# Stream 0's output projection between stream 1's head groups, in the PSUM banks of its own transposes, and stream 1's norms of A further forward

## What is computed

```python
mod = (silu(cvec) @ ada_w[l] + ada_b[l])          # six parts: sh1, sc1, g1, sh2, sc2, g2
xn = rms_norm(x, norm1_g[l]) * (1 + sc1) + sh1
aq, ak, av, bq, ..., cq, ckv, ckr = split(xn @ w_in)
qa, ka = rms_norm(aq), rms_norm(ak)               # "norms of A"; rotary in stream 1
oa = attention(qa, ka, va, sink)                  # A: 6 heads of 64; stream 1 sees 128 cached tokens too
ob = mlstm_mixer(bq, bk, bv, bo, bg, ...)         # B: 4 heads, both directions
oc = attention(qc, kc, vc)                        # C: low-rank q and kv, 6 heads of 96
x = x + g1 * (concat(oa, ob, oc) @ w_out[l])      # the output projection, 1024 x 1024
x = x + g2 * channel(rms_norm(x, norm2_g[l]) * (1 + sc2) + sh2)   # SwiGLU; layer 1: top 2 of 8 experts
```

## Time and profile before

| | us |
|---|---|
| median of 3 runs | 1760.65 (1760.57 to 1762.54) |
| the profiled execution, its own time | 1762.44 |
| its span in the trace | 1760.4 |
| PE busy | 1605.6 (91%) |
| DVE busy | 1197.8 (68%) |
| ACT busy | 919.7 (52%) |

### The profile page before, as it was taken

How to read it: one execution, slowest core, us unless ns; L and a number is a source line. 1 busy time by engine, 2 the same in 40 slices (tenths; PEclk the granted TensorE clock), 3 DMA queues, 4 the chain that set the end, 5 groups by cost and what they waited for, 6 DMA issues and landing times.

```text
span 1760.4 us, 20180 instructions
## 1 busy us (share of the span) xinstructions
PE 1605.6 (91%) x7272; PEld 1224.7 (70%) x7272; DVE 1197.8 (68%) x1311; ACT 919.7 (52%) x796; POOL 45.3 (3%) x83
## 2 busy tenths in 40 slices
PE   4987688999799759799999999999999999999996
PEld 1554346888655435678888888888888788788884
DVE  2244535444534553588888898889888888888885
ACT  1212124443221212377777777777777777777772
POOL 6000000000000000000000000000000000000000
PEclk8987698999898769799999999999999999999998
DMA  9958765555375754399999999899899999999990
GB/s 311 341 187 331 256 215 169 189 191 162 95 238 166 309 191 144 106 355 375 335 348 372 335 360 369 320 372 362 319 375 355 336 370 338 345 375 330 347 387 29
DMA packets 168331, 502.14 MB, mean 285 GB/s; under 512 B 9840, under 2 KB 52992, under 8 KB 162144
## 3 DMA queue, kind: packets, MB, share of 16 engines
q1 hardware_dynamic: 163952, 492.34, 77.2%
q0 software_dynamic: 3712, 7.55, 1.6%
q10 hardware_dynamic: 624, 1.68, 0.2%
HBM read 499.73 MB, written 1.81 MB: 285 GB/s over the span
## 4 chain that ended last, share of the span: by engine, by line
PE 88%; DVE 6%; ACT 2%; DMA 2%; issue 1%; ACTq 0%; POOLq 0%; POOL 0%; DVEq 0%
PE PS L531 21%; PE PS L533 21%; PE PS L532 21%; PE PS L605 6%; PE PS L537 5%; PE PS L820 3%; PE PS L914 2%; PE PS L921 2%; PE PS L551 2%; DMA ring<-in_w_in 2%; PE PS L619 1%; PE PS L635 1%; ACT arena L1135 1%; PE PS L723 1%; DVE small L1504 1%
## 5 line engine op out<-in xcount | busy, mean ns | idle before, releaser
L1872 DVE TENSOR_TENSOR parts<-ring,parts 128x2048 fp32r<-128x2048 f32 x336 | 766.0, 2291 | 133.3 <-ACT parts L1301 133.0
L1301 ACT ACTIVATE parts<-ring 128x2048 fp32r<-128x2048 f32 x336 | 643.8, 1919 | 250.9 <-PE PS L533 250.8
L531 PE MATMUL PS<-parts 128*128 128x512 f32 x1608 | 641.9, 399 | 13.2 <-DVE parts L1416 7.2
L533 PE MATMUL PS<-parts 128*128 128x512 f32 x1608 | 630.0, 392 | 0.0
L532 PE MATMUL PS<-parts 128*128 128x512 f32 x1608 | 629.7, 392 | 0.0
L531 PEld LDWEIGHTS PS<-parts 128*128 128x128 f32 x1608 | 303.5, 189 | 83.9 <-issue 8.6
L532 PEld LDWEIGHTS PS<-parts 128*128 128x128 f32 x1608 | 303.9, 189 | 65.8 <-issue 3.8
L533 PEld LDWEIGHTS PS<-parts 128*128 128x128 f32 x1608 | 303.5, 189 | 65.1
L605 PE MATMUL PS<-ring,xnT 128*128 128x420 f32 (+1 forms) x320 | 126.4, 550 | 4.2 <-ACT xnT L1110 3.7
L1416 DVE TENSOR_TENSOR parts<-ring,parts 128x2048 fp32r<-128x2048 f32 x33 | 75.4, 2288 | 52.0 <-PE PS L533 50.6
L605 PEld LDWEIGHTS PS<-ring,xnT 128*128 128x128 f32 x320 | 63.5, 204 | 56.7 <-issue 49.6
(11 more groups left out here) (278 smaller groups left out, 993.3 us busy)
## 6 DMA issues: line engine op xcount, KB each, us to landing
ring<-in_moe_w SPq DMA_DIRECT2D x336, 1024.0 KB, 6.5
ring<-in_ada_w SPq DMA_DIRECT2D x48, 1024.0 KB, 10.5
ring<-in_w_in SPq DMA_DIRECT2D x32, 840.0 KB, 6.1
ring<-in_ffn_w SPq DMA_DIRECT2D x44, 512.0 KB, 4.3
ring<-in_w_out SPq DMA_DIRECT2D x16, 1024.0 KB, 5.9
ring<-in_ffn_w SPq DMA_DIRECT2D x11, 1024.0 KB, 4.8
ring<-in_w_in SPq DMA_DIRECT2D x8, 832.0 KB, 4.8
gate<-gate_rows POOLq DMA_DIRECT2D x8, 512.0 KB, 6.1
```

The costliest lines, as they stand in the source:

```text
L531: mm(out, s_hi, m_hi, start=start, stop=False)
L533: return mm(out, s_lo, m_hi, start=False, stop=stop)
L1301: A(w_hi(j), slot(n), ACT.Copy).then_inc(hi_ready, 1)
L1872: TT(w_lo(j, 3), slot(W0 + j), w_hi(j).bitcast(f32), ALU.subtract).then_inc(split_done, 1)
```

## The change

It does four things.

The pieces of `o0` move: two of them (the transposes and the first projection half) to between the third and fourth piece of `B1`, two behind the third piece of `C1`, the last behind its fifth. Stream 0's projection goes to banks 0 and 1, those of its own transposes (`bank(6 * s + n)`: 0 and 1 for stream 0, 6 and 7 for stream 1 as before), so it needn't wait for the modulation; the wait for `turned_out` passes to stream 1.

The residual becomes a generator of its own, `residuals`, token `r0`, two pieces, which run in front of the last piece of `C1`.

`n1` moves forward from behind the fifth piece of `C0` to between the second and third of `B0`, and the `a` pieces at the end of PHASE_1 are dealt out anew: five of them before the fourth piece of `C0` instead of three, one instead of three before the fifth, two behind it as before.

In PHASE_2 the `a` pieces shift too: a fourth before `A1`'s third piece, one instead of two behind `B1`'s third, one before `C1`'s fifth instead of three (layer 0), with two behind it.

```diff
-A0 i1 A0 i1 A0 i1 A0 B0 i1 B0 i1 B0 i1 i1 B0 B0 t0 i1 C0 t0 i1 C0 t0 i1 C0 a a a C0 g1 a a a C0 n1 a a C0 a C0
+A0 i1 A0 i1 A0 i1 A0 B0 i1 B0 i1 n1 B0 i1 i1 B0 B0 t0 i1 C0 t0 i1 C0 t0 i1 C0 a a a a a C0 g1 a C0 a a C0 a C0
...
-o0 o0 C1 o0 C1 o0 o0
+A1 l1 a A1 a c1 a a A1 a A1 B1 a B1 a B1 a o0 o0 B1 B1 a C1 t1 a C1 t1 t1 a C1 o0 a o0 a a C1 a C1 a a o0 C1 r0 r0 a C1
...
-                if s == 0:
+                if s == 1:
                     wait("turned_out", early_of[l])
...
-                        last = mm(bank(4 * s + 2 + n), t[:, a:a + 128], w[:, k, :],
+                        last = mm(bank(6 * s + n), t[:, a:a + 128], w[:, k, :],
...
                 v.tensor_copy(R(s, QKT + 512, 512), bank(4 * s + 1)).then_inc(Q["oT_d"], 1)
                 yield
+                for _ in range(4):
+                    yield
+
+            def residuals(l, s):
                 for n in range(2):
-                    yield
                     if n == 0:
                         dve.wait_ge(gate_in, 32 * gates_by(3 * l + 1))
                     summed(dve, first["out", l, s, 2 * n + 1])
-                    residual(l, 0, s, n, bank(4 * s + 2 + n), R(s, SQ, 512))
+                    residual(l, 0, s, n, bank(6 * s + n), R(s, SQ, 512))
                     yield
...
-                for _ in out1:
+                for _ in residuals(l, 1):
                     pass
```

More of the change, by code:

```diff
@@ L39 @@
 PHASE_1 = """
-A0 i1 A0 i1 A0 i1 A0 B0 i1 B0 i1 B0 i1 i1 B0 B0 t0 i1 C0 t0 i1 C0 t0 i1 C0 a a a C0 g1 a a a C0 n1 a a C0 a C0
+A0 i1 A0 i1 A0 i1 A0 B0 i1 B0 i1 n1 B0 i1 i1 B0 B0 t0 i1 C0 t0 i1 C0 t0 i1 C0 a a a a a C0 g1 a C0 a a C0 a C0
 """
 PHASE_2 = {0: """
-A1 l1 a A1 a c1 a A1 a A1 B1 a B1 a B1 a a B1 B1 a C1 t1 a C1 t1 t1 a a C1 a a C1 a a a C1 a
-o0 o0 C1 o0 C1 o0 o0
+A1 l1 a A1 a c1 a a A1 a A1 B1 a B1 a B1 a o0 o0 B1 B1 a C1 t1 a C1 t1 t1 a C1 o0 a o0 a a C1 a C1 a a o0 C1 r0 r0 a C1
 """, 1: """
-A1 l1 a A1 a c1 a A1 A1 B1 a B1 a B1 a a B1 B1 C1 t1 a C1 t1 t1 a C1 C1
-o0 o0 C1 o0 C1 o0 C1 o0
+A1 l1 a A1 a c1 a A1 a A1 B1 a B1 a B1 o0 o0 B1 B1 C1 t1 a C1 t1 t1 C1 o0 a o0 C1 a C1 o0 C1 r0 r0 C1
 """}
@@ L323, in build_program @@
             assert [at_piece[x] for x in ("A0", "A1", "B0", "B1", "C0", "C1")] == [3, 3, 4, 4, 6, 6]
-            assert [at_piece[x] for x in ("t0", "t1", "n1", "g1", "l1", "c1")] == [2, 2, 0, 0, 0, 0]
+            assert [at_piece[x] for x in ("t0", "t1", "n1", "g1", "l1", "c1")] == [2, 2, 0, 0, 0, 0] and at_piece["r0"] == 1
             for i in range(4):
@@ L1738, in out_proj @@
                     summed(dve, first["out", l, s, 2 * n + 1])
-                    residual(l, 0, s, n, bank(4 * s + 2 + n), R(s, SQ, 512))
+                    residual(l, 0, s, n, bank(6 * s + n), R(s, SQ, 512))
                     yield
             def mixer(l, ada):
-                pieces = {"a": ada, "o0": out_proj(l, 0), "t0": tail_B(l, 0), "t1": tail_B(l, 1),
+                pieces = {"a": ada, "o0": out_proj(l, 0), "r0": residuals(l, 0), "t0": tail_B(l, 0), "t1": tail_B(l, 1),
                           "A0": group_A(l, 0), "B0": group_B(l, 0), "C0": group_C(l, 0),
```

## The result

| | before | after |
|---|---|---|
| median of the runs, us | 1760.82 (1760.57 to 1762.54) | 1715.86 (1706.02 to 1721.4) |
| ratio | | 0.9737 [0.9691, 0.9782] |
| profiled execution, its own time | 1762.44 | 1714.65 |
| its span | 1760.4 | 1712.6 |
| PE busy | 1605.6 | 1588.9 |

The changed kernel is faster by 45 us, 2.6%. Forecast were 36, and a range from 1715 to 1743. The work is the same, and still PE was busy for 16.7 us less: many of its instructions ran at the other clock level. The four runs of the changed kernel lie further apart than those of before, and their order is that of their clocks: 1706.02 at 0.967, 1714.65 and 1717.06 at 0.959, 1721.4 at 0.954.

The account below looks back on a forecast made before the run. No engine bounds the end of PHASE_1; a chain through PE, DVE and ACT does. Terms of -20.9 us (layer 0) and -14.8 (layer 1), together -35.7 on 1762.44, give 1726.7, as median 1725; range 1715 to 1743.

Parts of the forecast that it names:

- The end of PHASE_1: C's 12 transposes to the multiplication with the values: earlier start by the waits, -7.3 us in each layer.
- the two halves in the gap of C's norm: Stream 1's wait for C's norm: two projection halves fit at cost 0, with 3.4 us to spare in layer 0.
- T16 to scores: Group C's sixteen transposes to its scores: fewer pieces between, -1.5 us in layer 0, -4.6 in layer 1.
- scores to projection: Group C's scores to stream 1's projection, the largest term: -14.6 us in layer 0, -5.4 in layer 1.
- `norms_A` at no cost: DVE in group B: `norms_A` makes it 3.3 us late, covered by its idle there, so cost nothing.
- Rival (2): `norms_A` isn't covered in its new place: +3.3 us in each layer, 1732 us; chance 0.08.
- 1 us for that and what follows: From the values to M (group B's L706, before L708): multiplication at the higher clock level and what follows, -1 us per layer.
- the first half's +3.5: M to kv (C's third piece): half between B's third and fourth piece delays stream 1, +3.5 us per layer, lower end 1.
- denser work ahead of L723 and L729 may keep the clock up and give some back: Group B behind the first half: a kept clock may return part of its cost, so the lower end is 1 us.
- (1): Every moved half runs at the lower level, 1.2 GHz: 15 us lost in all, 1740 us; chance 0.12.
- (3): FFN and experts start by something else than PE's arrival, so PHASE_2's gain counts for nothing: 1745 us; chance 0.04.
- (5): Slower: halves wait for queued weight loads, a stall up to 17.5 us; 1795 us at worst; chance 0.03.

Follow-up runs that it names:

- e1: Kernel before with the new PHASE_1 alone (`n1` forward, `a` pieces dealt anew): 1747.68 us, ratio 0.9915.
- e2: Changed kernel with the old PHASE_1 (`n1` and its `a` pieces as before), everything else changed: 1738.14 us, ratio 0.9865.
- e4: Changed kernel with its first projection half behind C's third piece instead of in group B: 1713.22 us, ratio 0.9748.
- e6: Changed kernel with 3 (layer 0) and 5 (layer 1) useless matmuls in stream 1's wait for C's norm: 1709.98 us, ratio 0.9713.
- e8: Changed kernel with the two residual pieces `r0` behind C1's last piece instead of ahead of it: 1721.5 us, ratio 0.9766.
- e12: Changed kernel with PHASE_1's `a` pieces dealt as before, `n1` still moved: 1717.26 us, ratio 0.9754.
- e7: Changed kernel with useless matmuls in seven of PE's remaining waits, those of e6 among them: 1704.54 us, ratio 0.9685.
- e10: e7 with e4's place for the first half, 2 and 4 useless matmuls before L721's wait, 0 and 2 before C's norm: 1697.63 us, ratio 0.9638.
- e9: Kernel before with 12 and 14 useless matmuls in stream 1's wait for C's norm (layers 0 and 1): 1754.62 us, ratio 0.9966.
- e5: Kernel before with 8 and 9 useless matmuls in stream 1's wait for C's norm (layers 0 and 1): 1760.51 us, ratio 0.9995.
- e11: e7 with 1 and 3 more useless matmuls where the first half waits for ACT's copy of the transposed `o`: 1702.49 us, ratio 0.9676.

## Why the prediction was right and wrong

**Right: the waits.** The end of PHASE_1 (-7.42 and -8.24 for -7.3), the two halves in the gap of C's norm (3.48 us to spare, forecast 3.4), T16 to scores (-1.17, -4.52 for -1.5, -4.6) and the largest term, scores to projection (-15.06, -5.11 for -14.6, -5.4). That e1 and e2 together measured 35.7 us, the forecast sum, is luck: e2's 22.6 us hold a gain of clock, and the two parts don't add up.

**Nearly right: `norms_A` at no cost.** DVE in group B of stream 0, layer 0, as the earlier trace rows:

```profile
98.64 0.16 DVE L1593 COPY small<-PS 128x8 f32<-128x8 f32 x1
101.77 0.16 DVE L1605 TENSOR_TENSOR small<-small,PS 128x8 f32<-128x8 f32 x1 [0.70 <-PE PS L715]
102.60 1.28 DVE L1615 TENSOR_TENSOR arena<-arena,PS 128x512 f32<-128x512 f32 x2 [0.39 <-ACT xr L1171]
```

The idle of 4.43 is gone, and of the 5.23 us 0.70 is left. DVE is 2.90 us later at L1593 (98.64 less 95.74) and 1.64 earlier at L1605 (101.77 for 103.41): PE had taken 5.91 us for the two input projection pieces there instead of 7.39. PE's wait for the product is 2.20 us instead of 1.72, so about 0.5 us was lost. In layer 1 of e1, where the two pieces took 7.58 us, PE's wait is 1.72 as before, and nothing was lost. Rival (2) had 3.3.

**Wrong: the clock, in three steps.** Two terms of the sum and the range failed. "1 us for that and what follows" was forecast at -2 us in the two layers and came to -5.9; the first half's +3.5 per layer was forecast at +7 and came to +0.35. Both were sized as if the instructions beside the filled waits kept nearly the durations they had before. So stream 1's projection starts 26.1 us earlier in layer 0 and 47.9 in layer 1, where 21 and 36 were forecast.

First, "I add 1 us for that and what follows", per layer, for the clock behind the wait that goes. The stretch it covers, values to M, changed by +0.16 and -6.03. In layer 1 the twelve transposes of stream 1's group A cut it into two parts. PE before:

```profile
593.74 2.66 PE L635 MATMUL PS<-arena 128*128 128x64 f32 x12
...
609.36 1.53 PE L537 MATMUL PS<-cst,arena 128*128 128x128 f32 x12 [1.86 <-ACT small L1138]
612.00 0.44 PE L635 MATMUL PS<-arena 128*128 128x64 f32 x2 [1.11 <-ACT arena L1143]
...
614.48 0.64 PE L635 MATMUL PS<-arena 128*128 128x64 f32 x2
...
622.31 2.03 PE L708 MATMUL PS<-MFB,cst 8*128 8x128 f32 x16
```

After:

```profile
559.72 1.55 PE L633 MATMUL PS<-arena 128*128 128x64 f32 x12 [0.25 <-ACT arena L1141]
...
570.82 2.31 PE L535 MATMUL PS<-cst,arena 128*128 128x128 f32 x12 [3.44 <-ACT small L1136]
573.07 1.91 PE L549 MATMUL PS<-ring,cT 128*32 128x512 f32 x8
574.90 0.44 PE L633 MATMUL PS<-arena 128*128 128x64 f32 x2
...
582.26 2.03 PE L706 MATMUL PS<-MFB,cst 8*128 8x128 f32 x16
```

The first part takes 15.62 us before and 11.10 after, and 11.10 in e1 too: 4.5 us come from the new PHASE_1, right behind the wait that it takes away. The second part takes 12.95 us before, 11.44 after, but 16.46 in e1: without more the 4.5 us are mostly lost again. What differs between e1 and after is the `a` piece that the change puts before A1's last piece in layer 1, where it fills ACT's 1.11 us; e2, which has that piece and the old PHASE_1, takes 11.30. The whole stretch takes 28.57 us before, 27.56 with the new PHASE_1 alone (e1), 25.16 with the piece but the old PHASE_1 (e2) and 22.54 with both. The granted clock from values to M went from 0.64 (593.70 to 622.30) to 0.92 (559.70 to 582.30); e1 was at 0.69. So the size of "what follows" was wrong for the first part, and the prediction didn't cost the piece at all; it saw it as 0.96 us of work that moves. e4, e6, e8 and e12, which keep the piece, take 21.1 to 23.5 us; e7 and e10, which also have two useless matmuls ahead of A's transposes, 21.1. In layer 0 the same instructions from values to M take 25.38 us in after, 22.51 in e12 and 21.10 in e6: +0.16 was the slow end of a spread.

Second, the first half at +3.5 with a lower end of 1. Its price up to L721 was +2.72 and +4.13, near the forecast. But "denser work ahead of L723 and L729 may keep the clock up and give some back" gave back 4.05 us in layer 0 and 2.4 in layer 1 by group C's third piece (in layer 0 one `a` piece less stands in there, but a wait of 0.76 us for ACT takes its place); e4 shows both sides of this trade, and its sum is nil. The net was -1.3 and +1.7, and the lower end of 1 should have been -1 or so. The -1.3 was on the lucky side: from M to kv e8, e12, e6 and e2 have the same instructions in layer 0, and against the kernel before they stand at -1.4, +1.7, +1.6 and +1.3. This term carries 6.7 us of the 12 that the trace has beyond the sum, the first one 3.9; the rest is 1 us here and there, among them the starts of both layers.

Third, the range: its lower end took in better PHASE_1 and B terms, but only by 8.4 us, and no clock gain outside of the stretches that were edited. One kernel's own runs spread over 15 us with the clock.

**The rivals.** (1), every moved half at the lower level, didn't come in this execution, where one of eight ran partly at it: 3.70, 3.60, 3.70 and 3.70 in layer 0; 5.13, 3.60, 3.70 and 3.60 in layer 1. But it is no fixed property: e6 has the same instructions as after up to that point, and its first half took 6.73 (169.31, wait 1.49) against 3.70, while it had gained 4.2 us just before it. It happens in some executions, and is part of the spread. (3) is out: from layer 1's norm transposes to the end it is 1047.8 us in both kernels, so the earlier arrival counts in full. (5): PE does wait for weights, 0.91 and 1.42 us in layer 0, 0.60 and 2.65 in layer 1, but in the head groups only for the five pieces of PHASE_1. In layer 1 that cost 1.05 us at C's transposes, in layer 0 nothing. The rule cited in the prediction weighed on the wrong side: I read it as a warning for pieces that are dealt between waits. The Trainium skill's "TensorE: Matmul & The Clock Gate", Part 1, states it of activity as such: the slow clock is the default, and activity releases it. The traces agree where it is applied to the instructions behind a wait that is filled: 3.65 us for the sixteen transposes in before, 1.95 in e9.

**Open.** What decides, at a given place, whether the clock falls in one execution and not in another isn't settled. e5 and e9 show only that with 4.48 us of wait left in that place the transposes behind it took 3.65 us, and with 1.05 us left 1.95.

## What to carry to other kernels

A piece of work laid into a wait can be worth more than the wait that it fills, and the gain can be lost again a few microseconds later if the next wait stays open (e1 against the changed kernel): read the durations of the instructions behind the wait too, and compare them with the same instruction elsewhere in the trace (1.95 or 3.65, 3.60 or 6.52). Where a kernel is a chain of short pieces, cost every edit twice, once in waits and once in clock, and widen the range on the good side too when the edit fills gaps. Where nothing useful fits, try useless matmuls that are sized to fill nearly all of the wait; here 8 and 9 of them brought nothing, 12 and 14 did. And take several executions: single traces of the same instructions differ by 1 to 4 us in a stretch here.

## What the runs showed of the hardware

Useless matmuls made the kernel faster: by 6.6 us on the kernel before (0.9966 [0.9953, 0.998]), and by 16 to 19 us on the changed one with its first half later (e4, 0.9748 [0.972, 0.9776], to e10, 0.9638 [0.9619, 0.9657]). PE's instructions ran at 2.4 instead of 1.2 GHz more often: the granted clock over the long window is 0.87 before, 0.90 in e9, 0.91 in e4 and 0.94 in e10. In one place, filling a wait of 11.54 us down to 4.48 gave nothing, and down to 1.05 the transposes behind it took 1.95 us instead of 3.65. The same instructions can run at either level in different executions: the first half took 3.70 us in after and 6.73 in e6. So whole times can spread: 1706 to 1721 us for the changed kernel, 1692 to 1713 for e11, against 1757.7 to 1763.2 for the kernel before over 11 runs. It need not show in few runs: e12's five lie between 1716.6 and 1717.9.
